# One expert slot per group in place of two, in a two-layer diffusion backbone with gathered experts

## The reference

```python
def block(args):
    xb, eb, gb = args
    a = jax.nn.gelu(jnp.einsum('tkd,td->tk', u_tab[eb], xb), approximate=False)
    return jnp.einsum('tk,tkd->td', gb * a, v_tab[eb])
```

## Time and profile before

| | |
|---|---|
| median of 3 runs | 5946.48 us (5943.82 to 5949.09) |
| the profiled execution | 5943.26 us; its span 5941.0 us |
| busy, share of the span | PE 62%, PEld 43%, DVE 49%, ACT 28%, POOL 23% |
| HBM | 1706.68 MB read, 19.23 MB written, 291 GB/s over the span |
| gathers | 1342.26 MB in 1280 gathers, median 12.5 us from issue to landing |
| mean granted clock of PE | 0.73 of full speed |

### The profile page before, as it was taken

How to read it: one execution, slowest core, us unless ns; L and a number is a source line. 1 busy time by engine, 2 the same in 40 slices (tenths; PEclk the granted TensorE clock), 3 DMA queues, 4 the chain that set the end, 5 groups by cost and what they waited for, 6 DMA issues and landing times.

```text
span 5941.0 us, 64624 instructions
## 1 busy us (share of the span) xinstructions
PE 3655.9 (62%) x22248; PEld 2530.1 (43%) x22248; DVE 2908.1 (49%) x6855; ACT 1675.6 (28%) x4743; POOL 1395.3 (23%) x1297
## 2 busy tenths in 40 slices
PE   3889457788785675436455556778435787433333
PEld 1677445566664453224133235677213565311111
DVE  0321747634447544764444444321765444864444
ACT  0200127332432342233322222200224253222222
POOL 0000013212221232223334331000233222133443
PEclk7779779858887787667576668769657798655555
DMA  6434358748896898779999995114788899689998
GB/s 258 151 130 163 116 203 315 288 178 307 321 392 232 296 408 360 268 280 385 382 402 409 407 405 233 40 55 152 263 314 339 312 376 357 224 344 407 408 412 360
DMA packets 326553, 1730.30 MB, mean 291 GB/s; under 512 B 95984, under 2 KB 108624, under 8 KB 138832
## 3 DMA queue, kind: packets, MB, share of 16 engines
q0 software_dynamic: 184320, 1342.26, 57.1%
q1 hardware_dynamic: 120272, 351.64, 16.3%
q10 hardware_dynamic: 21632, 32.27, 1.9%
HBM read 1706.68 MB, written 19.23 MB: 291 GB/s over the span
## 4 chain that ended last, share of the span: by engine, by line
PE 39%; DMA 27%; DVE 15%; ACT 6%; issue 4%; DVEq 4%; ACTq 3%; POOL 2%; SPq 1%; PEldq 0%; POOLq 0%; PEld 0%
PE psum L471 26%; DMA arena<-in_uv,arena 22%; PE psum L819 5%; DVE arena L2095 4%; POOL arena L1135 2%; DVE arena L2002 1%; DVE arena L1995 1%; DMA arena<-in_w_ada 1%; DVE arena L1996 1%; PE psum L431 1%; PE psum L652 1%; PE psum L653 1%; ACT L1507 1%; ACT arena L1514 1%; ACT arena L1230 1%
## 5 line engine op out<-in xcount | busy, mean ns | idle before, releaser
L1135 POOL DMA_INDIRECT arena<-in_uv,arena x1280 | 1391.0, 1087 | 4511.8 <-PE psum L819 2985.4
L2095 DVE CUSTOM_DVE_ANT_0 arena<-arena 128x1024 f32<-128x1024 f32 x1280 | 1556.7, 1228 | 1378.9 <-DMA arena<-in_uv,arena 1324.2
L471 PE MATMUL psum<-arena 128*128 128x256 f32 (+2 forms) x8480 | 2027.5, 399 | 185.7 <-DVEq L1534 62.4
L819 PE MATMUL psum<-arena 128*32 128x256 f32 x10240 | 994.9, 527 | 1548.2 <-ACTq L1515 1535.0
L471 PEld LDWEIGHTS psum<-arena 128*128 128x128 f32 (+1 forms) x8480 | 1676.0, 202 | 564.6 <-issue 101.7
L819 PEld LDWEIGHTS psum<-arena 128*32 128x32 f32 x10240 | 336.4, 137 | 2116.4 <-ACTq L1515 1738.6
L1507 ACT ACTIVATE arena<-arena 128x2 f32<-128x2 f32 x640 | 131.0, 205 | 1824.1 <-DVEq L2097 1598.0
L1514 ACT ACTIVATE arena<-arena 128x32 f32<-128x32 f32 x1280 | 341.7, 314 | 45.3 <-issue 1.1
L431 PE MATMUL psum<-arena 128*128 128x128 f32 (+1 forms) x680 | 134.3, 355 | 337.3 <-DVE arena L1593 117.5
L1511 ACT ACTIVATE arena<-arena 128x1 f32<-128x1 f32 x1280 | 307.5, 287 | 45.8 <-issue 1.7
L431 PEld LDWEIGHTS psum<-arena 128*128 128x128 f32 (+1 forms) x680 | 101.9, 184 | 381.4 <-issue 166.2
(11 more groups left out here) (211 smaller groups left out, 2756.1 us busy)
## 6 DMA issues: line engine op xcount, KB each, us to landing
arena<-in_w_in SPq DMA_DIRECT2D x92, 1024.0 KB, 7.4
arena<-in_w_mix SPq DMA_DIRECT2D x120, 768.0 KB, 8.3
arena<-in_w_ada SPq DMA_DIRECT2D x32, 1536.0 KB, 16.3
arena<-in_w_wq SPq DMA_DIRECT2D x40, 1152.0 KB, 5.4
arena<-in_w_wo SPq DMA_DIRECT2D x20, 1024.0 KB, 8.9
arena<-in_uv,arena POOLq DMA_INDIRECT x1280, 12.5
arena<-h_rows ACTq DMA_DIRECT2D x160, 128.0 KB, 6.8
arena<-ada_rows SPq DMA_DIRECT2D x15, 512.0 KB, 7.7
```

Source lines behind the costliest of these rows:

```text
L471: ins = mm(out, a, b, start=(i == 0), stop=(i == last))
L819: ins = mm(acc_bank(u)[32 * q:32 * q + 32, gg * 256:gg * 256 + 256], DIAG[:, c, :], RING[:, sl, D + q * 256:D + (q + 1) * 256], start=(h, ...
L1135: pool.indirect_dma_start(RING[:, sl, :], None, io["uv"], bass.IndirectOffsetOnAxis(PICKED_U[b][:, h_, tg, a:a + 1], 0)).then_inc(gathered ...
L2095: V_.tensor_tensor_reduce(out=RING[:, sl, 0:D], in0=RING[:, sl, 0:D], in1=XT[:, gg, :], scale=1.0, scalar=0.0, op0=ALU.mult, op1=ALU.add, ...
```

## The change

`GS` becomes 1. A group is one slot, a unit has 64 groups, a head of a unit 8. The ring keeps its 8 slots of 1 MB. `LAG_ACT`, `LAG_PE` and `LAG_TAIL` stay 1, 2 and 3, in groups. Gelu is one column wide and is issued 1280 times in place of 640; so are the drains with `dots`, `diag` and `slots_free`; POOL waits before each gather. The dots, copies, diagonals, gathers and expert matmuls stay the same in number and size. Leads and cuts in `schedule` are doubled so that they stand for the same slots, except the lead of `final 4`, which stays 16 groups.

```diff
@@ -21,7 +21,7 @@
-GS = 2
+GS = 1
@@ -130,9 +130,9 @@
     cut = 4 * GROUPS
-    return [(a, [], 0), (b, p0, 0), (c1, p1[:cut], 0), (c2, p1[cut:], 8), (d, [], 0), (e1, p2[:cut], 0),
-            ([("final", 2, ())], p2[cut:cut + 64], 8), ([("final", 3, ())], p2[cut + 64:cut + 80], 8),
-            ([("final", 4, ())], p2[cut + 80:], 16), ([("final", 5, ())], [], 0)]
+    return [(a, [], 0), (b, p0, 0), (c1, p1[:cut], 0), (c2, p1[cut:], 16), (d, [], 0), (e1, p2[:cut], 0),
+            ([("final", 2, ())], p2[cut:cut + 128], 16), ([("final", 3, ())], p2[cut + 128:cut + 160], 16),
+            ([("final", 4, ())], p2[cut + 160:], 16), ([("final", 5, ())], [], 0)]
```

## The result

The changed kernel takes **6436.02 us** (median; 6431.69 to 6439.55) against 5947.56 us (5943.82 to 5949.09) of the kernel before, measured beside it: ratio 1.0822, 95% interval 1.0803 to 1.0841. It is slower by 488 us, where +340 and at most 6400 us were forecast. The direction and the stages were right; the time lies above the range.

A forecast was written before the change was run, and what follows sets the result against it. No single engine was taken as the bound: transfers, PE, or program order and latency between engines, by stage. Terms 91 + 129 + 54 + 17 + 54 + 30 - 35 = +340 us gave about 6286 us, range 6095 to 6400.

The forecast's parts named there:

- merge: Three stages beside gathers: PE's second group behind a step waits about 2.2 us for ACT; +91 us, bounds 0 and +200.
- route: Four stages: PE's next queries wait for dots behind DVE's head work, lengthening heads; +129 us, bounds +80 and +160.
- attention: Units beside gathers get two or three single-slot groups, PE's scores come later, 9.4 us per unit; +54 us, bounds 0 and +115.
- mLSTM: Three to four groups behind a unit instead of one to two add ACT and PE chains; +17 us, bounds 0 and +50.
- dense stages bound by PE: qkv, mlp, mc of both layers: PE has almost no idle time to hide added waits; +54 us, bounds +10 and +90.
- deeper ring: Six gathers under way instead of four help where transfers bind but are not full; -35 us, bounds 0 and -83.
- PE's clock: Granted clock share falls some tenths in merge and attention where waits come in; +30 us, bounds 0 and +90.
- the rival in which the ring decides: Ties hidden behind DVE's wait for gathers; slots freed earlier land gathers earlier in every stage; 5863 us, chance 0.05.
- The ring absorbing the ties: Merge and dense stages cost nothing more; only route, attention and mLSTM pay; +160 us, 6106 us, chance 0.13.
- The clock rival: PE held at the lower clock level through merge, attention and mc stages; 6407 us, chance 0.09.
- the lag in slots does not matter: DVE runs ahead anyway, so the time stays within 0.2% of now; chance 0.03.
- its 87 us: Extra drain for some 63 exposed ACT table switches in merge and attention, estimated from the skill page, left out of the sum.

The follow-up runs named there:

- e11: Changed kernel plus zero-weight products on PE ahead of only the second group behind each step of dense stages and merge: 6319.88 us, 1.0628 of the kernel before.
- e4: Changed kernel plus 24 small zero-weight products on PE ahead of every group behind a merge step except the first: 6424.45 us, 1.081 of the kernel before.
- e7: Changed kernel with LAG_ACT, LAG_PE, LAG_TAIL at 1, 4, 5 in place of 1, 2, 3: 5962.22 us, 1.0028 of the kernel before.
- e1: Changed kernel with lags 2, 4, 6 in place of 1, 2, 3, so lags in slots are as before: 5999.22 us, 1.0099 of the kernel before.
- e2: Kernel before (pairs) with LAG_PE 1 in place of 2, the lag in slots of the changed kernel: 6685.9 us, 1.1249 of the kernel before.
- e5: Changed kernel with lags 2, 4, 6 and the earlier kernel's quotas and final 4's lead doubled: 5965.83 us, 1.0035 of the kernel before.
- e9: Changed kernel with LAG_ACT, LAG_PE, LAG_TAIL at 1, 5, 6 in place of 1, 2, 3: 5930.53 us, 0.9975 of the kernel before.

## Why the prediction was right or wrong

By its own terms, from the stage times (predicted, then measured in the profiled executions; their spans differ by 493 us):

| term | predicted | measured |
|---|---|---|
| merge | +91 | +155 |
| route | +129 | +127 |
| attention | +54 | +81 |
| mLSTM | +17 | +38 |
| dense stages bound by PE (layer 0, and mc(1,2)) | +54 | +88 |
| deeper ring (layer-1 stages in the stream, last stream) | -35 | about 0 |
| PE's clock | +30 | inside the terms above |

**The failed step is the term "PE's clock": +30, bounds 0 and +90.** It was put in as one lump, argued from mean clocks of whole stages, where it had to be worked out per step. A wait of 2.2 us in each merge step lengthens nearly all sets of 24 products behind it from 5.47 us to between 6.3 and 7.7. Over the 24 steps of a stage these sets took 156.7 us in merge(0,1) and 162.7 in merge(1,2), against 132.7 and 136.0 before: 51 us more, and 9 more in merge(0,2). The merge term was short by 64. PE's busy time, which has the expert matmuls in it too, says it again: +30 in merge(0,1) (193.58 to 223.46) and +37 in merge(1,2), of which the split into single slots makes some 8.

For attention, e11 lifts the clock to 0.94 in da(0) and finds da(0) at 184.4 us and da(1,2) at 100.4; 146.6 + 39 and 86.5 + 15, the prediction's own terms without a clock, are 185.6 and 101.5. For merge, e4 finds 267.4 and 295.4 with the clock lifted, of which the prediction's waits alone (+35 and +29 with the w_o steps' share of 17) make about 269 and 288. In mc(0) PE's busy time grew by 9 us and its idle time by 23, of which 22 had been predicted. **So the waits of merge, attention and mc(0) were priced about right, and the slower products behind them were not priced.** (The fills lift the clock above that of the kernel before, 0.94 against 0.87 in da(0) and 0.96 against 0.90 in merge(1,2), so the close match is in part luck.)

Merge, attention, mLSTM and the dense stages came out 146 us over their terms. Of that, longer products make about 122: 60 in merge, 27 in attention, 14 in ml(0) and 21 in qkv, mlp and mc of layer 0, by PE's busy time in the last two. Only 30 had been set aside for it. The 116 over and the 35 that the ring did not give are the missing 150.

The trace of before had it to read only in part. In merge(0,2) there, PE behind one wait of 2.16 us, and behind the wait of the earlier trace rows:

```profile
2015.67 1.43 PE L819 MATMUL psum<-arena 128*32 128x256 f32 x16 [2.16 <-ACTq L1515]
2017.03 6.74 PE L471 MATMUL psum<-arena 128*128 128x256 f32 x24
...
2072.50 5.47 PE L471 MATMUL psum<-arena 128*128 128x256 f32 x24
```

Of the seven waits of 2.16 us in that stage four have 5.47 us behind them and three 6.15 to 6.74, 0.4 us too long on average. In the changed kernel such a wait stands in every step of merge(1,2); 21 of its 24 sets take 6.3 to 7.7 us, and still three behind a wait of 2.2 us take 5.47. One step could not give the size; all of them could have given a range, 0.4 to 1.7 us for each of the 40 new waits, 16 to 68 us in merge alone.

**Route was right** in mechanism, and in its sum; its four parts were off by 5 to 7 us each and cancel (+50, +43, +19 and +15 for +57, +48, +14 and +10), which is luck. Heads of route(0,1) and (1,2), DVE of the changed kernel:

```profile
2054.57 0.19 DVE L2041 CAST arena<-arena 128x64 f32<-128x64 uint32 x1 [0.16 <-issue]
2085.57 0.19 DVE L2041 CAST arena<-arena 128x64 f32<-128x64 uint32 x1 [0.17 <-issue]
...
5491.82 0.20 DVE L2041 CAST arena<-arena 128x64 f32<-128x64 uint32 x1 [0.17 <-issue]
5524.88 0.19 DVE L2041 CAST arena<-arena 128x64 f32<-128x64 uint32 x1 [0.16 <-issue]
```

31.0 and 33.1 us, where 30.8 and 32.2 were forecast; those of route(0,2) are 37.6 and 39.5 for 36.4. It came out right although the clock fell here too (0.71 to 0.67); that a head's chain is mostly DVE's searches would explain it, and was not tested. Most heads with five and eight slots came out up to 3 us longer than forecast. In route(0,1) the forecast took all seven intervals from 22.6 us; the first, behind three groups, was 31.4 before and became 32.3, and that is the 7 us that are missing there.

**Attention** was right in its place and short in its size. DVE of the changed kernel, one maximum per unit:

```profile
982.08 1.76 DVE L1649 TENSOR_REDUCE arena<-psum 128x2 f32<-128x1536 f32 x1 [3.69 <-PE psum L557]
993.63 1.76 DVE L1649 TENSOR_REDUCE arena<-psum 128x2 f32<-128x1536 f32 x1 [4.47 <-PE psum L557]
1004.40 1.76 DVE L1649 TENSOR_REDUCE arena<-psum 128x2 f32<-128x1536 f32 x1 [4.17 <-PE psum L557]
```

11.6 and 10.8 us in place of 9.4, with DVE now waiting some 4 us for PE's scores, where in the regular units before it had no wait.

**mLSTM** missed its term by half. It was reckoned as waits alone, +17, within 0 to 50; PE was busy 155.62 us after and 141.14 before (clock 0.50 and 0.56), 14 of the 29 us. The clock is worth more than these 14: with the fill of e11 ml(0) takes 166.6 us, less than the 175.1 of the kernel before, and e7 has it at 155.9 without a fill. So ml(0) loses to the low clock and to waits in the kernel before, too.

**The ring** gave nothing. In the two streams the gathers are limited by the transfers at 396 to 401 GB/s, before and after. The change did deepen the queue in the last stream, from 4.8 gathers under way on average to 6.1, and the rate stayed (398 and 396 GB/s; 696.4 and 700.0 us). The lump of -35 had been read off slices at 407 GB/s, as if more depth could bring every stage there; it did not. Of the gathers' share, the rival in which the ring decides had its place right, DVE's wait for a gather, but that wait went from 1324.2 to 859.7 us, which fits DVE being made late by the ties and not gathers coming early, since no stage of the table got shorter.

**The other rivals.** The ring absorbing the ties fell to the same trace: merge(0,1) moves 297 GB/s, so no transfer covers anything there. The clock rival (6407 us, 0.09) named the right term and was still 29 us too low; its condition, the lower level throughout merge, attention and mc, did not come about (0.82 to 0.86, 0.74 to 0.76 and 0.93). That the lag in slots does not matter is out by e1 and e2.

**The two pages.** ACT's table load takes 1.28 us and Gelu starts 0.01 us after its end (5199.24 and 5200.53 above), as in the earlier trace rows. The Trainium skill, "ScalarE: Activation LUTs", section "What ACT_TABLE_LOAD costs", adds 1.38 us of drain to each switch; this trace again does not show it, and the 2.19 us of PE's wait leave no room for it (0.38 + 1.28 + 0.20 + 0.29 + 0.32 less PE's 0.64 are 1.83, and the gaps make the rest). Leaving its 87 us out was right for the mechanism, though a sum with them, 6373 us, would have been nearer to the result, for a reason that is not there. The same skill's "Perfetto Trace Analysis", section "Optimizing Scalar/DVE Operations", has it that breaking up instructions may complete work sooner where engines cause bubbles on others. Here the break-up alone, the order being kept in slots, is worth +0.35% (e5), and with a lag of five slots the kernel is 0.25% faster (e9), which need not be the break-up's doing; the bubbles were made and removed by the lag.

## What to carry to other kernels

Where an order is written out by hand, a lag belongs to the amount of work between two engines' programs, in slots or in time; halve the unit and the lag in units must double with it. Count how many units stand behind a dense step: as many as the distance to ACT are free, then PE waits for ACT, and from the distance to DVE on it waits for DVE. Price a short wait of TensorE with what comes behind it, by comparing the same group of products behind a wait and behind none, over all steps of a stage: a single step can show nothing (5.47 us behind the wait of the earlier trace rows), and a stage's mean clock hides it.

## What the runs showed of the hardware

- In merge(1,2), where TensorE waits 2.2 us in every step of about 10.5 us, 21 of the 24 sets of 24 float32 products of 128x256 take 6.3 to 7.7 us against 5.47 us without waits, and the stage's granted clock goes from 0.90 to 0.84, between the levels of 1.2 and 2.4 GHz. Products of zeros in the gap bring it to 0.96. Single waits of 2.16 us in the kernel before have 5.47 us behind them in four of seven cases.
- In ml(0) the granted clock is 0.50 after the change, the lower level throughout, though PE is busy 76% of the stage. With products of zeros ahead of the second group behind each unit it is 0.76, and the stage is 38 us shorter.
- In the last stream 4.8 gathers of 1 MB under way on average move 398 GB/s and 6.1 move 396: more depth brought nothing.
